# U and V rows of the PEER experts side by side in one table, gathered by one 8 KB row per expert slot through a ring of eight slots

## The reference

```python
def peer_ffn(h, wq, subkeys, u, v):
    q = (xt @ wq).reshape(T, PEER_HEADS, 2, PEER_HALF)
    s = jnp.einsum('thpc,hpnc->thpn', q, subkeys).astype(jnp.float32)
    s_top, i_top = lax.top_k(s, PEER_TOPK)            # 16 of 128 keys in each half
    ...                                               # 16 x 16 sums, top 16 of them
    gates = jax.nn.softmax(best, axis=-1).astype(h.dtype)
    ...
    def block(args):
        xb, eb, gb = args                             # 128 tokens, 128 experts each
        ub = u[eb]
        vb = v[eb]
        act = jax.nn.gelu(jnp.einsum('cd,ced->ce', xb, ub), approximate=False) * gb
        return jnp.einsum('ce,ced->cd', act, vb)
```

## Time and profile before

| | |
|---|---|
| Median of 3 runs | 2038.15 us (2032.91 to 2041.07) |
| Time of the profiled execution | 2035.14 us |
| Its span, first to last instruction | 2033.2 us |
| Mean granted clock of TensorE, share of full speed | 0.935 |
| Busy: TensorE, VectorE, ScalarE, GpSimd | 1648.9, 1223.1, 693.9, 660.7 us |
| First gather issued; last V row landed and used | 383.3 us; 1177.9 us |

### The profile page before, as it was taken

The page is one execution under the profiler, slowest core; times in us unless marked ns, Lnnn a source line. Parts: engine busy times, 40 slices in busy tenths (PEclk is TensorE's granted clock), DMA queues, the critical chain, the costliest instruction groups (busy, mean ns, idle before and its releaser), DMA issues.

```text
span 2033.2 us, 23626 instructions
## 1 busy us (share of the span) xinstructions
PE 1648.9 (81%) x9301; PEld 1238.9 (61%) x9301; DVE 1223.1 (60%) x2437; ACT 693.9 (34%) x1222; POOL 660.7 (32%) x583
## 2 busy tenths in 40 slices
PE   5788798457786677766777778787999998999999
PEld 4778798434442222222233256786999986569999
DVE  4665466475767676744454455754677555756774
ACT  4535544122221121211111143322554443545542
POOL 1100011267767777777777700210100010000000
PEclk9898899778999998899989998898999999999999
DMA  6322242479999989999999922111444552014443
GB/s 230 125 83 104 103 167 95 164 261 320 350 335 362 386 322 342 359 371 350 379 385 387 355 96 104 52 54 42 149 183 142 169 187 83 22 57 151 184 152 121
DMA packets 100295, 421.15 MB, mean 207 GB/s; under 512 B 12116, under 2 KB 15448, under 8 KB 85080
## 3 DMA queue, kind: packets, MB, share of 16 engines
q0 software_dynamic: 73728, 268.47, 35.5%
q1 hardware_dynamic: 23936, 148.70, 20.4%
q10 hardware_dynamic: 2520, 2.47, 0.4%
HBM read 418.54 MB, written 1.05 MB: 206 GB/s over the span
## 4 chain that ended last, share of the span: by engine, by line
PE 49%; DVE 20%; DMA 11%; POOL 8%; ACT 6%; issue 5%; another core or an unknown queue 1%; ACTq 0%; DVEq 0%; POOLq 0%
PE bank L302 47%; DMA ur<-in_u,idx 6%; DVE ur L1281 5%; POOL vr L1426 4%; DMA vr<-in_v,idx 4%; POOL ur L1426 4%; DVE wp L358 2%; DVE cacc L318 1%; ACT wp L310 1%; ACT L314 1%; DVE whl L358 1%; PE bank L2382 1%; PE bank L307 1%; ACT wf L310 1%
## 5 line engine op out<-in xcount | busy, mean ns | idle before, releaser
L302 PE MATMUL bank<-vr,dg 128*128 128x512 f32 x1000 | 501.3, 639 | 191.7 <-DMA vr<-in_v,idx 95.0
L302 PEld LDWEIGHTS bank<-vr,dg 128*128 128x128 f32 x1000 | 186.2, 200 | 497.9 <-issue 405.6
L1281 DVE CUSTOM_DVE_ANT_0 ur<-ur,htok 128x1024 f32<-128x1024 f32 x256 | 312.9, 1222 | 217.5 <-DMA ur<-in_u,idx 182.2
L1426 POOL DMA_INDIRECT vr<-in_v,idx x256 | 299.8, 1171 | 122.3 <-PE bank L302 61.5
L1426 POOL DMA_INDIRECT ur<-in_u,idx x256 | 282.6, 1104 | 117.3 <-issue 57.0
L469 POOL TENSOR_TENSOR sqT<-sqT 128x256 f32<-128x256 f32 (+1 forms) x42 | 49.2, 1170 | 724.7 <-ACT sqT L314 722.2
L358 DVE TENSOR_TENSOR whl<-slabs,whl 128x2048 fp32r<-128x2048 f32 (+1 forms) x70 | 148.2, 2117 | 56.0 <-ACT whl L310 55.7
L358 DVE TENSOR_TENSOR wp<-slabs,wp 128x2048 fp32r<-128x2048 f32 (+1 forms) x61 | 132.9, 2179 | 72.9 <-ACT wp L310 72.6
L302 PE MATMUL bank<-hn,whl 128*128 128x272 f32 (+2 forms) x1392 | 173.3, 285 | 0.0
L302 PEld LDWEIGHTS bank<-hn,whl 128*128 128x128 f32 x1392 | 171.8, 189 | 0.1
L310 ACT ACTIVATE whl<-slabs 128x2048 fp32r<-128x2048 f32 (+1 forms) x70 | 122.7, 1754 | 108.4 <-PE bank L302 108.4
(11 more groups left out here) (353 smaller groups left out, 2303.5 us busy)
## 6 DMA issues: line engine op xcount, KB each, us to landing
slabs<-in_up SPq DMA_DIRECT2D x44, 1024.0 KB
slabs<-in_w_in SPq DMA_DIRECT2D x28, 1024.0 KB
slabs<-in_dn SPq DMA_DIRECT2D x32, 704.0 KB
slabs<-in_wkv SPq DMA_DIRECT2D x8, 1024.0 KB
slabs<-in_w_out SPq DMA_DIRECT2D x8, 1024.0 KB
slabs<-in_pq SPq DMA_DIRECT2D x8, 1024.0 KB
slabs<-in_wq SPq DMA_DIRECT2D x4, 1024.0 KB
slabs<-in_wo SPq DMA_DIRECT2D x4, 1024.0 KB
```

The source lines that it names most:

```text
L302: ins = T.e.matmul(pr[2] if len(pr) > 2 else out, pr[0], pr[1], start=(start and k == 0), stop=(stop and k == len(pairs) - 1), skip_group_ ...
L1281: V.e.tensor_tensor_reduce(u_, u_, htok[:, n, :], 1.0, 0.0, ALU.mult, ALU.add, dots[:, n, e_:e_ + 1]).then_inc(*V.up("dot", q))
L1426: G.e.indirect_dma_start(buf[q % used][:, :], None, d[x[0]][:, :], bass.IndirectOffsetOnAxis(ap=idx[:, n, e_:e_ + 1], axis=0)).then_inc(lo ...
```

## The change

U and V are laid side by side in one table `uv` of 16384 rows of 2048 floats. One gather of slot q fetches 128 rows of 8 KB into one of eight buffers `uv`. It waits until TensorE has finished slot q - 8. VectorE takes the dot product over the first half of the buffer straight into `acts`. ScalarE then takes the gelu of that one column, multiplies it by its gate and makes the diagonal, slot by slot; the ring of diagonals has three places. TensorE multiplies by the second half of the buffer, for all 256 slots; `BY_VECTOR`, the groups, `dots` and `vacc` go. The lag between `("u", q)` and `("v", q)` is 2 slots.

A new entry `("parts", h)` carries the split of a head's weight slab, placed ahead of the first six choice steps that come before that head's scores. Behind each of the first 16 slots stand three entries instead of two. Some small buffers now lie inside `s2`, and both sides of a choice share one buffer `oneh`, so the second side waits for the first.

```diff
-        NU, NV_, GRP, LAG = 8, 6, 8, 12
+        NU, NDG, LAG = 8, 3, 2
...
-            ur = [sbuf(ph, f"ur{i}", [P, D]) for i in range(NU)]
-            vr = [sbuf(ph, f"vr{i}", [P, D]) for i in range(NV_)]
-            dg = [sbuf(ph, f"dg{i}", [P, P]) for i in range(8)]
+            uv = [sbuf(ph, f"uv{i}", [P, 2 * D]) for i in range(NU)]
+            dg = [sbuf(ph, f"dg{i}", [P, P]) for i in range(NDG)]
...
             for h in range(1, 7):
-                todo += scores_of(h + 1) + choice_of(0, h)
+                steps = choice_of(0, h)
+                todo += [("parts", h + 1)] + steps[:6] + scores_of(h + 1) + steps[6:]
...
                     out.append(("u", q))
-                    pump(2)
-                    if q in STARTS:
-                        out.append(("act", q))
+                    pump(3 if q < 16 else 2)
...
-                o3 = oneh[:, side, :].rearrange("p (k i) -> p k i", k=16)
+                o3 = oneh[:, :].rearrange("p (k i) -> p k i", k=16)
                 if k == 0:
-                    V.wait_ge(*V.at(*key, "pf"))
+                    V.wait_ge(*V.at(*key, "eid", 0) if side else V.at(*key, "pf"))
...
-                    V.wait_ge(s_u[q % NU], 16 * (q // NU + 1))
+                    V.wait_ge(s_uv[q % NU], 16 * (q // NU + 1))
                     V.wait_ge(*A.at("htok", n, 1))
-                    u_ = ur[q % NU][:, :]
-                    V.e.tensor_tensor_reduce(u_, u_, htok[:, n, :], 1.0, 0.0, ALU.mult, ALU.add, dots[:, n, e_:e_ + 1]).then_inc(*V.up("dot", q))
+                    u_ = uv[q % NU][:, 0:D]
+                    V.e.tensor_tensor_reduce(u_, u_, htok[:, n, :], 1.0, 0.0, ALU.mult, ALU.add, acts[:, n, e_:e_ + 1]).then_inc(*V.up("dot", q))
...
-                elif x[0] == "act":
-                    n, e_ = divmod(x[1], P)
-                    gs = slice(STARTS[x[1]] % P, e_ + 1)
-                    A.wait_ge(*V.at("dot", x[1]))
-                    act(acts[:, n, gs], dots[:, n, gs], ACT.Gelu).then_inc(*A.up("gelu", x[1]))
-                elif x[0] == "v" and x[1] not in BY_VECTOR:
+                elif x[0] == "v":
                     q = x[1]
                     n, e_ = divmod(q, P)
-                    A.wait_ge(*V.at("act", GROUP_OF[q]))
-                    if q > 7:
-                        A.wait_ge(*T.at("y", q - 8, 1))
-                    act(dg[q % 8][:, :], ident, ACT.Copy, scale=acts[:, n, e_:e_ + 1]).then_inc(*A.up("diag", q))
+                    a_ = acts[:, n, e_:e_ + 1]
+                    A.wait_ge(*V.at("dot", q))
+                    act(a_, a_, ACT.Gelu).then_inc(*A.up("gelu", q))
+                    A.wait_ge(*A.at("gelu", q))
+                    A.wait_ge(*V.at("gat", n, e_ // 16))
+                    act(a_, a_, ACT.Copy, scale=gat[:, n, e_ // 16, e_ % 16:e_ % 16 + 1]).then_inc(*A.up("act", q))
+                    A.wait_ge(*A.at("act", q))
+                    if q >= NDG:
+                        A.wait_ge(*T.at("y", q - NDG, 1))
+                    act(dg[q % NDG][:, :], ident, ACT.Copy, scale=acts[:, n, e_:e_ + 1]).then_inc(*A.up("diag", q))
...
             for x in PEER:
-                if x[0] in ("u", "v"):
+                if x[0] == "u":
                     q = x[1]
                     n, e_ = divmod(q, P)
-                    buf, used, loads = (ur, NU, s_u) if x[0] == "u" else (vr, NV_, s_w)
                     G.wait_ge(*V.at("idx", n, e_ // 16))
-                    if q >= used:
-                        G.wait_ge(*(V.at("dot", q - NU) if x[0] == "u" else
-                                    V.at("vacc", q - NV_) if q - NV_ in BY_VECTOR else T.at("y", q - NV_, 1)))
-                    G.e.indirect_dma_start(buf[q % used][:, :], None, d[x[0]][:, :],
-                                           bass.IndirectOffsetOnAxis(ap=idx[:, n, e_:e_ + 1], axis=0)).then_inc(loads[q % used], 16)
+                    if q >= NU:
+                        G.wait_ge(*T.at("y", q - NU, 1))
+                    G.e.indirect_dma_start(uv[q % NU][:, :], None, d["uv"][:, :],
+                                           bass.IndirectOffsetOnAxis(ap=idx[:, n, e_:e_ + 1], axis=0)).then_inc(s_uv[q % NU], 16)
```

More of the change, by code:

```diff
@@ L207, in build @@
             cand = sbuf(ph, "cand", [P, 256])
-            oneh = sbuf(ph, "oneh", [P, 2, 256])
-            ur = [sbuf(ph, f"ur{i}", [P, D]) for i in range(NU)]
-            vr = [sbuf(ph, f"vr{i}", [P, D]) for i in range(NV_)]
-            dg = [sbuf(ph, f"dg{i}", [P, P]) for i in range(8)]
+            oneh = sbuf(ph, "oneh", [P, 256])
+            uv = [sbuf(ph, f"uv{i}", [P, 2 * D]) for i in range(NU)]
+            dg = [sbuf(ph, f"dg{i}", [P, P]) for i in range(NDG)]
             htok = sbuf(ph, "htok", [P, 2, D])
@@ L214, in build @@
             gat = sbuf(ph, "gat", [P, 2, 8, 16])
-            dots = sbuf(ph, "dots", [P, 2, P])
             acts = sbuf(ph, "acts", [P, 2, P])
             sub = sbuf(ph, "sub", [P, 16, P])
-            sv_ = sbuf(ph, "sv_", [P, 2, 16])
+            sv_, pf, eid = (s2[:, 1, P + 32 * i:P + 32 * i + 32].rearrange("p (a b) -> p a b", a=2) for i in range(3))
+            best = s2[:, 1, P + 96:P + 112]
             si = sbuf(ph, "si", [P, 2, 16], U32)
             sif = sbuf(ph, "sif", [P, 2, 16])
-            best = sbuf(ph, "best", [P, 16])
             pos = sbuf(ph, "pos", [P, 16], U32)
             pij = sbuf(ph, "pij", [P, 2, 16], U32)
-            pf = sbuf(ph, "pf", [P, 2, 16])
-            eid = sbuf(ph, "eid", [P, 2, 16])
             sm = sbuf(ph, "sm", [P, 2])
@@ L280, in build @@
         s_slab = [sem(f"slab{i}_loaded") for i in range(NSLOT)]
-        s_u = [sem(f"u{i}_gathered") for i in range(NU)]
-        s_w = [sem(f"v{i}_gathered") for i in range(NV_)]
+        s_uv = [sem(f"uv{i}_gathered") for i in range(NU)]
         def C(name, lo=0, hi=None):
@@ L1125, in build @@
         EARLY = 2 * P - 50
[L1127 to L1132, removed]
         SQE = ytok[:, 0:8 * 144].rearrange("p (c t) -> p c t", c=NC)
@@ L1263, in peer_vector @@
                     h, j = x[1], x[2]
-                    if j == 0:
+                    if j == 0 and h < 2:
                         ahead(N_PQ + h, split_vector)
@@ L1270, in peer_vector @@
                         scaled_vector(qpb[h % 2][:, j, :], pbank("pq", h, j)[:, 0:T1], "np", T1).then_inc(*V.up("ev", "pq", h, j))
+                elif x[0] == "parts":
+                    ahead(N_PQ + x[1], split_vector)
                 elif x[0] == "tokens":
@@ L1277, in peer_vector @@
                     n, e_ = divmod(q, P)
-                    V.wait_ge(s_u[q % NU], 16 * (q // NU + 1))
+                    V.wait_ge(s_uv[q % NU], 16 * (q // NU + 1))
                     V.wait_ge(*A.at("htok", n, 1))
-                    u_ = ur[q % NU][:, :]
-                    V.e.tensor_tensor_reduce(u_, u_, htok[:, n, :], 1.0, 0.0, ALU.mult, ALU.add, dots[:, n, e_:e_ + 1]).then_inc(*V.up("dot", q))
+                    u_ = uv[q % NU][:, 0:D]
+                    V.e.tensor_tensor_reduce(u_, u_, htok[:, n, :], 1.0, 0.0, ALU.mult, ALU.add, acts[:, n, e_:e_ + 1]).then_inc(*V.up("dot", q))
                 elif x[0] == "early":
                     early_vector(x[1])
-                elif x[0] == "act":
-                    n, e_ = divmod(x[1], P)
-                    gs = slice(STARTS[x[1]] % P, e_ + 1)
[L1287 to L1304, removed]
+                elif x[0] == "v" and x[1] % P == P - 1:
+                    added_vector(x[1] // P)
         def added_vector(n):
@@ L1309, in added_vector @@
                 hs = slice(half * 512, half * 512 + 512)
[L1310 to L1317, removed]
+                V.wait_ge(*T.at("y", n * P + P - 1, half))
+                V.wait_ge(*(T.at("early") if n else T.at("htok", 1, 1)))
+                V.e.tensor_copy(ytok[:, hs], B[4 + 2 * n + half][:, :]).then_inc(*V.up("ytok", n, half))
             for half in range(2):
@@ L1321, in added_vector @@
                 V.e.tensor_tensor(xs, B[half][:, :].rearrange("p (c t) -> p c t", c=4), xs, ALU.add).then_inc(*V.up("peer_x", n, half))
-        def last_of(n):
-            return max(q for q in range(n * P, n * P + P) if q not in BY_VECTOR)
         def early_vector(k):
@@ L1376, in peer_scalar @@
                 if x[0] == "scores" and x[2] < 2:
-                    if x[2] == 0:
+                    if x[2] == 0 and x[1] < 2:
                         ahead(N_PQ + x[1], split_scalar)
+                elif x[0] == "parts":
+                    ahead(N_PQ + x[1], split_scalar)
                 elif x[0] == "scores":
@@ L1468, in peer_tensor @@
                     n, e_ = divmod(q, P)
[L1469 to L1475, removed]
+                    T.wait_ge(*A.at("diag", q))
+                    T.wait_ge(*A.at("htok", 1, 1))
+                    T.wait_ge(s_uv[q % NU], 16 * (q // NU + 1))
+                    for half in range(2):
+                        mm(B[4 + 2 * n + half][:, :], [(dg[q % NDG][:, :], uv[q % NU][:, D + half * 512:D + half * 512 + 512])],
```

(4 more changed lines are left out.)

3 lines of the change are left out of this document (removed).

## The result

The changed kernel takes 1926.33 us (median of four runs, 1925.66 to 1934.15), the kernel before 2036.07 on the same chip. The ratio is 0.9455, 95% interval 0.9428 to 0.9481. It is 110 us faster where I had forecast 29.

The account below looks back on a forecast made before the run. It took the gathers' DMA bytes at 370 GB/s as the bound, with GpSimd second; -18 - 11 - 3 + 3 = -29 us from 2035.14 gives 2006, median 2009, range 1982 to 2046.

Parts of the forecast that it names:

- the first division: Gather stretch, 383 to 1180 us: rate over DMA share gives 370 GB/s, so bytes need 749 us, leaving 48 to win.
- Half the gathers: Middle stretch: 256 fewer gathers free 375 us of hidden GpSimd time and take back 11 us, bounds 0 and 16.5.
- Price of a byte: Gather stretch: 8 KB rows move at the same price per byte as 4 KB rows, 0 us.
- The dearer row: Rival for the gather stretch: long rows cost more per byte, +26 us, total 2035; chance 0.10.
- The cheaper row: Rival for the gather stretch: long rows cost less per byte, -30 us, total 1979; chance 0.06.
- The start: Stretch up to 600 us: the new order and ring take back 18 of 28 us idle, bounds 0 and 25.
- The load of TensorE, the extra products, VectorE: Gather stretch: TensorE's load fits narrowly, its six more products cost 12 us, VectorE saves about 12, all hidden.
- ScalarE: Gather stretch: gelus wait behind the exp once per head, some 2 x 2.83 + 3 us, covered by 11 us.
- The end: End of the gathers: whole slots save 3 us, the longer tail behind the last landing costs 3 us.
- The dry ring: Rival at heads 2 to 7: projection and exp holds together empty the eight buffers, 2073 us; chance 0.17.
- My last sign of being wrong: Gather slots: the prediction fails above all if slots are held much longer than 11 us after issue.
- The memory limit of 358 GB/s: Rival for the gather stretch: memory, not issue, sets 358 GB/s, about -9 us, 2029 with the tail; chance 0.10.

Follow-up runs that it names:

- rates: A separate kernel, run once, that only gathers random 4 KB or 8 KB rows with varying numbers in flight, with and without VectorE dot products; 317 to 422 GB/s among its phases.
- slower_issue: The changed kernel with twelve tiny memsets on GpSimd ahead of each gather; 2086.89 us, ratio 1.0237.
- before_short_dots: The kernel before, with dot products over only 32 of the 1024 columns; 2020.46 us, ratio 0.9904.
- old_order: The changed kernel with the list in its old order: split right ahead of its scores, scores ahead of choice steps, two entries behind each slot; 1942.80 us, ratio 0.9536.
- exp_later: The changed kernel with ScalarE's exp of the gates behind step 13 of a choice in place of step 10; 1909.89 us, ratio 0.9373.
- ring6: The changed kernel with six buffers of 8 KB in place of eight; 1993.85 us, ratio 0.9778.
- ring4: The changed kernel with four buffers of 8 KB in place of eight; 2224.32 us, ratio 1.0915.

## Why the prediction was wrong, point by point

**The step that failed** is the first division: "Divided by the share, the rate is 348/0.94 = 370 GB/s, so the bytes alone need 749 us. The 48 us above that are what any reordering can win." From it the price of a byte was taken as 0, and GpSimd as "the second pacemaker". The stretch with gathers fell by 107 us, from 797 to 690. Of this the idle share gives 48 - 0.03 x 690 = 27 us. The busy time gives 749 - 0.97 x 690 = 80 us, for the same bytes, and for these I had no term. `rates` shows why: at 2 MB in flight the share is 0.94 to 0.97 and the rate 340 to 356; it takes more in flight to see what the engines can do. The kernel before had 2.2 MB in flight. What held it there, by its own trace, was GpSimd's queue: 2.82 us of work in a slot of 2.92. I had both numbers, and read the 0.10 between them as slack when it was the 16 us of waits in 400. So GpSimd was the first pacemaker: `slower_issue` shows that its pace alone can bring the rate down and the packets up, with long rows and the new ring in place. It wasn't alone: `before_short_dots` takes 46 of 400 us off the gathers and gains only 18 us in all, as stops of GpSimd take their place. How the 80 us split between its pace and such stops is open. What the runs do show is that the new ring and order without the single gather give 13 us, and with it 110.

**Half the gathers.** Right in kind: one packet a row, 36,864 packets, 299 us of GpSimd for 280. Wrong in worth: I gave it 11 us, all in the middle. The middle went from 364 to 413 GB/s, which over 550 us and 200 MB is 65 us.

**Price of a byte.** The dearer row didn't come. The cheaper row is worth 3% in `rates`, 20 us of 690. My lower bound of -30 would have covered that. (The page gives 0.355 x 2033 = 722 us of gathers where I wrote 716, and 4.5% of that is 32, not 30; neither matters here.) The bound came from the best window of the stretch itself, which was under the same pace. The slices of 10 us at 414 to 420 GB/s, shown above, would have given a better one.

**The start.** 0.03 x 215 = 6 us idle in place of 28, so 22 for my 18; `old_order` gives the order 16. TensorE's waits for the split fell from 45.7 us in five cases to one of 16.0 us, at the first projection of the stretch, and VectorE's waits for projections from 40.7 us in eleven to 9.5 in five.

**The load of TensorE, the extra products, VectorE.** Said to be hidden. From 800 to 1050 us, at 427 GB/s and a share of 1.01, they are; for the stretch ahead of that no run tests them by themselves.

**ScalarE.** The hold per exp was described rightly (some 8.7 us; measured 5.74 and two table loads of 1.28, with the exp itself 8.6 from 723.78 to 732.42 us) and called covered. It wasn't quite: `exp_later` gains 16 us. With the engines able to do 427, eight buffers last 20 us and not 23.

**The end.** From the last use of a landed row to the next stage it took 6.75 us (1066.25 to 1073.00) where it had been 4.44 (1177.88 to 1182.32), +2.3 for my +3.

**The rivals.** The dry ring didn't come at eight buffers; `ring6` and `ring4` show it just below. My last sign of being wrong was badly chosen. The last slot was held 19 us from issue to the end of its product (1051.19 to 1070.51), far over 11, while the kernel gained: most of a hold is the queue ahead of the row, and a full queue is what was wanted. The memory limit of 358 GB/s is excluded by 427. Here the Trainium skill ("HBM Reference", the table of specifications and the sentence under it) has about 425 GB/s for a core that streams alone; the trace agrees with it, at 427. I had noted this as a reason against a rival, and not as one against my own 370.

## What to carry to other kernels

A DMA share near 1 doesn't mean that the DMA engines are the limit. Compare the issuing engine's time per transfer, its waits and fixed gaps included, with the time of a slot, and ask how many bytes are in flight; where the issue takes nearly all of the slot, larger transfers per instruction can pay twice, once in pace and once in the rate that a deep queue gives. An issuer needs a reserve over the transfer rate, or each stall is lost for good. A mean rate hides this, so look at short slices too: the best of them show what the engines can do. Once the rate is up, a ring lasts a shorter time and holds that it used to cover come to light.

## What the runs showed of the hardware that I had not expected

- Gathers of 4 KB rows moved 202 GB/s with two in flight (1 MB), 340 with four and 410 with sixteen allowed; 8 KB rows 356 with two and 422 with four or more. So 4 MB in flight were enough, 2 MB were not.
- At 202 GB/s the DMA share still read 0.67, at 356 it read 0.97, at 422 it read 1.01.
- A gather instruction took GpSimd 0.94 us for 128 rows of 4 KB and of 8 KB alike, and 0.30 us more before the next. Beside dot products of VectorE the mean rose to 67.29/40 = 1.68 us in the phase with 8 KB rows, and to 76.52/78 = 0.98 in the one with 4 KB rows, whose gathers follow each other at another beat.
- In the kernel before, 240 of the gathers issued from 400 to 1170 us began inside a dot product of VectorE. They took 1.32 us in the mean, and the median one ended 0.81 us after the dot product. Six began inside the 2.29 us `tensor_tensor` of 128x2048 that splits a slab, and those ended 0.80 us after it as well (1.90 us each). The 232 that began in none of VectorE's instructions took 0.94 us. `before_short_dots` brought the mean of all gathers from 600 to 1000 us from 1.11 to 0.945 us.
